# Feed-forward products that read the moving operand in groups of four columns from halves or quarters of the row

## The reference

```python
for layer in range(2):
    h = rmsnorm(x, mix_norm[layer])
    ...                                   # layer 0: gated conv and window attention; layer 1: spatial gating and latent attention
    x = x + y
    h = rmsnorm(x, ffn_norm[layer])
    gate, up = jnp.split(h @ w_ffn_in[layer], 2, axis=-1)      # (512, 1024) @ (1024, 5632)
    x = x + (jax.nn.silu(gate) * up) @ w_ffn_out[layer]        # (512, 2816) @ (2816, 1024)
```

## Time and profile before

| | us |
|---|---|
| median of 2 runs | 1114.61 |
| the runs | 1114.23 and 1114.98 |
| profiled execution: span, first to last instruction | 1112.0 |
| TensorE busy in it | 1102.9 (99%) |
| VectorE, ScalarE, GpSimd busy | 560.2, 420.4, 102.9 |

### The profile page before, as it was taken

How to read it: one execution, slowest core, us unless ns; L and a number is a source line. 1 busy time by engine, 2 the same in 40 slices (tenths; PEclk the granted TensorE clock), 3 DMA queues, 4 the chain that set the end, 5 groups by cost and what they waited for, 6 DMA issues and landing times. The chain is left out here.

```text
span 1112.0 us, 13661 instructions
## 1 busy us (share of the span) xinstructions
PE 1102.9 (99%) x5105; PEld 887.1 (80%) x5105; DVE 560.2 (50%) x784; ACT 420.4 (38%) x662; POOL 102.9 (9%) x126
## 2 busy tenths in 40 slices
PE   8999999999999999999999999999999999999998
PEld 7777788888888888888877766788888888888887
DVE  6678977434433433242466588656433433453321
ACT  5545445333322322231345567544322322332110
POOL 6000000001000100000002023000000100110000
PEclk9999999999999999999999999999999999999999
DMA  7422223333333233322233200223233333327431
GB/s 236 159 57 76 76 75 96 114 95 95 94 94 94 94 102 103 98 95 85 67 103 94 77 35 1 77 96 112 89 101 94 94 97 100 102 78 170 113 123 48
DMA packets 101289, 106.00 MB, mean 95 GB/s; under 512 B 26235, under 2 KB 77888, under 8 KB 101120
## 3 DMA queue, kind: packets, MB, share of 16 engines
q1 hardware_dynamic: 83536, 103.04, 29.8%
q10 hardware_dynamic: 16656, 2.10, 1.1%
q0 software_dynamic: 1056, 0.30, 0.1%
HBM read 101.23 MB, written 2.10 MB: 93 GB/s over the span
## 5 line engine op out<-in xcount | busy, mean ns | idle before, releaser
L1122 DVE TENSOR_TENSOR w_lo<-raw,w_hi 128x1024 fp32r<-128x1024 f32 (+2 forms) x192 | 224.6, 1176 | 419.1 <-ACT w_hi L697 416.3
L697 ACT ACTIVATE w_hi<-raw 128x1024 fp32r<-128x1024 f32 (+2 forms) x192 | 194.2, 1017 | 468.7 <-PE ps L1685 438.4
L1683 PE MATMUL ps<-h_hi,w_hi 128*128 128x512 f32 x912 | 359.7, 394 | 1.0 <-DVE h_lo L1146 1.0
L1685 PE MATMUL ps<-h_hi,w_lo 128*128 128x512 f32 x912 | 355.1, 389 | 0.0
L1684 PE MATMUL ps<-h_lo,w_hi 128*128 128x512 f32 x912 | 355.0, 389 | 0.0
L1683 PEld LDWEIGHTS ps<-h_hi,w_hi 128*128 128x128 f32 x912 | 171.3, 188 | 42.9 <-issue 6.7
L1684 PEld LDWEIGHTS ps<-h_lo,w_hi 128*128 128x128 f32 x912 | 171.2, 188 | 36.7 <-issue 1.7
L1685 PEld LDWEIGHTS ps<-h_hi,w_lo 128*128 128x128 f32 x912 | 171.2, 188 | 35.9
L581 POOL TENSOR_TENSOR ffn_t<-ffn_t,row_scale 128x512 f32<-128x512 f32 x40 | 51.0, 1295 | 614.2 <-ACT ffn_t L883 614.2
L1684 PE MATMUL ps<-w_lo,act_hi 128*128 128x512 f32 (+1 forms) x178 | 68.8, 387 | 0.0
L1685 PE MATMUL ps<-w_hi,act_lo 128*128 128x512 f32 (+1 forms) x178 | 68.8, 387 | 0.0
(11 more groups left out here) (283 smaller groups left out, 1173.4 us busy)
## 6 DMA issues: line engine op xcount, KB each, us to landing
raw<-in_w_ffn_in SPq DMA_DIRECT2D x88, 512.0 KB, 3.5
raw<-in_w_ffn_out SPq DMA_DIRECT2D x44, 512.0 KB, 3.7
raw<-in_e_w_in SPq DMA_DIRECT2D x17, 512.0 KB, 3.7
raw<-in_o_w_in SPq DMA_DIRECT2D x8, 512.0 KB, 3.6
raw<-in_o_w_out SPq DMA_DIRECT2D x8, 512.0 KB, 3.6
raw<-in_e_w_out SPq DMA_DIRECT2D x8, 256.0 KB, 3.9
raw<-in_e_w_out SPq DMA_DIRECT2D x4, 512.0 KB, 4.5
out_tok<-x_blocks ACTq DMA_DIRECT2D x16, 128.0 KB, 2.5
```

What stands on the lines that cost most here:

```text
L697: ins = act.activation(dst, src, ACT.Copy)
L1122: ins = TT(dst, src, high, ALU.subtract)
L1683: MM(dst, st_hi, mv_hi, start=start, stop=False)
L1685: return MM(dst, st_lo, mv_hi, start=False, stop=stop)
```

## The change

The rows of `h_hi` and `h_lo` are stored in another order in rounds 1 and 3, and read back through the same pattern, so that the array gets the columns in the old order. A row of 512 columns is seen as groups of four. In round 1 the groups go in turn to the first and the second half of the row, in round 3 in turn to the four quarters. For feature tiles 0 to 3 the groups run from the end of each half or quarter to its start, for tiles 4 to 7 from its start to its end. `h_order` is the pattern of the stored tile, `x_order` the same columns of `xT` in their own order. The moving operand of a feed-forward input matmul thereby has three levels: 4 columns side by side, a jump of 256 columns (1024 bytes) or 128 columns (512 bytes) to the next half or quarter, and a step of 4 columns up or down. `h_low` is issued once for each half or quarter, with the count of the semaphore on the last.

```diff
--- before.py
+++ after.py
@@ -39,6 +39,7 @@
 RAW_SLOTS = 2
 W_SLOTS = 4
 LEAD = W_SLOTS
+RUNS_BACK = {(1, 0): (2, True), (1, 1): (2, False), (3, 0): (4, True), (3, 1): (4, False)}
 
 
 E_Q, E_KV, E_AIN, E_AC, E_AB, E_OUT = 0, 4, 6, 10, 14, 18
@@ -650,6 +651,21 @@
     def h_gain(rnd, ft):
         return mix0_gain[:, ft:ft + 1] if rnd == 0 else g_col({1: G_FFN0, 2: G_MIX1, 3: G_FFN1}[rnd] + ft)
 
+    def h_order(tile, rnd, ft):
+
+        if rnd not in (1, 3):
+            return tile[:, ft, :]
+        parts, back = RUNS_BACK[rnd, ft // 4]
+        view = tile[:, ft, :].rearrange("p (b a i) -> p a b i", b=parts, i=4)
+        return view[:, ::-1, :, :] if back else view
+
+    def x_order(rnd, ft):
+
+        if rnd not in (1, 3):
+            return xT[:, ft, :]
+        parts, back = RUNS_BACK[rnd, ft // 4]
+        return xT[:, ft, :].rearrange("p (a b i) -> p a b i", b=parts, i=4)
+
     X_BANKS = (4, 5, 6, 7, 4, 5, 6, 7)
     V_BANKS = ((0, 2), (3, 3))
 
@@ -724,7 +740,7 @@
         def h_high(rnd, ft):
 
             act.wait_ge(x_ready, 8 * rnd + ft + 1)
-            act.activation(h_hi[:, ft, :], xT[:, ft, :], ACT.Copy, scale=h_gain(rnd, ft)).then_inc(h_hi_ready, 1)
+            act.activation(h_order(h_hi, rnd, ft), x_order(rnd, ft), ACT.Copy, scale=h_gain(rnd, ft)).then_inc(h_hi_ready, 1)
 
         def h_square(rnd, ft):
             f = 8 * rnd + ft
@@ -1143,8 +1159,15 @@
         def h_low(rnd, ft):
             f = 8 * rnd + ft
             dve.wait_ge(h_hi_ready, f + 1)
-            STT(out=h_lo[:, ft, :], in0=xT[:, ft, :] if rnd else ps[:, X_BANKS[ft], :], scalar=h_gain(rnd, ft), in1=h_hi[:, ft, :].bitcast(F32),
-                op0=ALU.mult, op1=ALU.subtract).then_inc(h_lo_ready, 1)
+            if rnd not in (1, 3):
+                STT(out=h_lo[:, ft, :], in0=xT[:, ft, :] if rnd else ps[:, X_BANKS[ft], :], scalar=h_gain(rnd, ft),
+                    in1=h_hi[:, ft, :].bitcast(F32), op0=ALU.mult, op1=ALU.subtract).then_inc(h_lo_ready, 1)
+                return
+            dst, src, high = h_order(h_lo, rnd, ft), x_order(rnd, ft), h_order(h_hi, rnd, ft).bitcast(F32)
+            for part in range(RUNS_BACK[rnd, ft // 4][0]):
+                ins = STT(out=dst[:, :, part, :], in0=src[:, :, part, :], scalar=h_gain(rnd, ft), in1=high[:, :, part, :],
+                          op0=ALU.mult, op1=ALU.subtract)
+            ins.then_inc(h_lo_ready, 1)
 
         def h_sum(rnd, ft):
             f = 8 * rnd + ft
@@ -1941,7 +1964,8 @@
 
             def half_group(n, j, b0, shift):
 
-                load(n + j, plain(256, 2), range(4 * (j // 2), 4 * (j // 2) + 4), H,
+                load(n + j, plain(256, 2), range(4 * (j // 2), 4 * (j // 2) + 4),
+                     lambda k: (h_order(h_hi, rnd, k), h_order(h_lo, rnd, k)),
                      (b0 + 2 * (j % 2), b0 + 2 * (j % 2) + 1), j < 2, j >= 2, shift)
 
             pe.wait_ge(x_ready, 8 * rnd + 4)
```

## The result

The changed kernel takes 1182.43 us (1182.31 and 1182.55) against 1114.61: ratio 1.0608, 95% interval 1.0577 to 1.0639, slower by 67.8 us. The span of its profiled execution is 1180.5 us, 68.5 over the one before.

What follows compares the result with a forecast made beforehand. TensorE, busy 99% of the 1112.0 us span, was taken as the bound. Zero for reads, `h_high` and clock plus 1.2 us for the `h_low` split, on the 1114.6 us median, gave 1115.8 us, own range 1113.8 to 1119.

Steps and rivals of the forecast that it cites:

- The read in groups of four: Main term, TensorE's 2112 feed-forward input matmuls: jumps in the moving read cost zero, bounded between a 28 us gain and +427 us.
- The signs of being wrong: Spacings differing between layers or tile directions, longer `h_high`, VectorE fixed part far from 0.13 us, or idle time inside groups.
- The argument from the spacing: TensorE matmul starts: 0.417 ns a column, one cycle at 2.4 GHz, plus fixed 0.0133 us; no delay inside a contiguous row.
- rival C: TensorE's moving reads: alternating halves hide some of the fixed 13.3 ns, all of it 28 us, giving 1088 us; chance 0.03.
- rival A: All 2112 matmuls: read port bubbles at jumps; one cycle each +113 us, 1229 us, or 1172 if half pay; chance 0.15.
- The split of `h_low`: VectorE: each extra piece pays 0.13 us (to 0.21) fixed; the sum is +1.2 us, ends 0 and +3.8.
- the hole at the mean of layer 1: TensorE waits 1.1 us before `mean` in layer 1's second half, as `h_low` pieces delay VectorE's last sum; high price 2.9.
- a semaphore's passage: 0.1 us added to the 1.1 us hole in the `h_low` split's sum of +1.2 us.
- `h_high`: ScalarE's 16 writes at permuted places: same count and elements, 0.72 us each, cost zero; even +0.3 us each is hidden.
- The clock: Granted clock 1.00 in both feed-forward stretches; values unchanged, only storage moves: zero.
- Rival B: Start of each matmul costs a few ns more, not growing with columns; 1119 to 1130 us; chance 0.05.

Runs made afterwards that it cites:

- e_turn1: Changed kernel with all h_hi and h_lo rows of layers 0 and 1 read as single columns in turn from two halves, forward: 1093.9 us, ratio 0.982 to kernel before.
- e_n256: Changed kernel with feed-forward input matmuls on the first 256 columns only; halves by four, plain, single columns from halves, quarters by four: 983.86 us.
- e_sweep: Changed kernel with groups of four, forward, from 8 and 16 parts (layer 0), 32 and 64 parts (layer 1): 1156.05 us.
- e_width: Changed kernel with forward groups of 8 and 16 columns, from halves in layer 0 and quarters in layer 1: 1135.77 us.
- e_split: Kernel before with only h_low cut into two (layer 0) or four (layer 1) instructions, rows in old order: 1115.53 us against 1114.39, ratio 1.001.
- e_best: Changed kernel with single columns from halves for h_hi and h_lo, plus act_hi and act_lo rows of layer 0's output products: 1088.35 us, ratio 0.9769 to kernel before.
- e_near: Changed kernel with single columns in turn from two neighbouring runs of 4 and 2 columns (layer 0), 8 and 64 (layer 1): 1098.73 us.
- e_swap: Changed kernel with directions exchanged: tiles 0 to 3 forward, 4 to 7 backward: 1181.32 us.
- e_ldw64: Changed kernel with 64 stationary columns instead of 128; layer 0 quarters and halves by four forward, layer 1 plain: 1149.18 us.
- e_wstep: Changed kernel with weights read every second column of 256; halves by four, plain, single columns from halves, quarters by four: 1151.33 us.
- e_step2: Changed kernel with every second column and backward singles from halves (layer 0), backward pairs from halves and backward groups of four from 32 parts (layer 1): 1282.45 us.
- e_back1: Changed kernel without halves or quarters: tiles 0 to 3 read backward in groups of four, tiles 4 to 7 plain: 1121.55 us.

## Why the prediction was wrong

**The step that failed is the main term**, "The read in groups of four": I took zero for 2112 matmuls, and it measured +21.7 ns (halves) and +42.0 ns (quarters) each, 67.3 us. The reason given, that all words of a group lie side by side and each is read once, is true and not what counts. The nearest rows were of other engines, at 64 columns a run, as the text said; the error was to let them and that reason set the value where the trace had nothing of its own. The signs of being wrong that the prediction named came true: the spacings differ between halves and quarters, and between backward and forward.

**The argument from the spacing was too strong.** The earlier trace rows do show 0.417 ns for each further column of a plain row, and 13.3 ns that don't grow with the columns. I took 0.417 ns for the length of one cycle (2.4 GHz is its inverse) and concluded that nothing is lost inside a row; that was an estimate from this one difference. From it I concluded that nothing in the fixed 13.3 ns depends on addresses (rival C) and that moving on to the next four columns is free wherever they lie (against rival A). Both fell: single columns from two streams take 10.8 of the 13.3 ns away (e_turn1), and e_n256 shows the groups' price growing with the columns, from 6.7 to 23.5 ns for halves.

**Rival A is the nearest to the case**, with 0.15. Its place holds: all 2112 matmuls pay, in the read of the moving operand. Its mechanism, one lost step at every jump, does not: groups of four 64 bytes apart jump as often and pay nothing (223.4 ns, e_sweep), and halving the jumps of quarters takes nine tenths of their price away (from 41.2 to 4.4 ns, e_width). Its price was mis-sized too, since I let it begin at a column's whole 0.417 ns for every jump (1229 us, or 1172 for half the forms). Spread over the 128 jumps, the price is 0.17 ns a jump for halves (21.7 by 128) and 0.33 for quarters (42.0 by 128). That the measured 1182 lies near the 1172 is chance: all forms pay, each less than 0.417 ns a jump.

**The split of `h_low`** was right in its working: 0.13 us a piece forecast, 0.13 measured (0.39 for three more pieces); +1.2 us forecast, +1.1 alone; the hole at the mean of layer 1 forecast at 1.1 us, 0.99 found. The 0.1 us that the sum adds for a semaphore's passage came from no row; in e_split the last sum of squares ends at 760.67 us and the mean starts at 760.82, 0.15 us later. In the full change that hole is covered, and no cost of the split is seen on TensorE. **`h_high`** at zero was right (722 ns, 719 before). **The clock** at 1.00 was right.

**Rival B**, a fixed start price of the three-level pattern, is not the case: the pattern costs nothing at 64 bytes (223.4 ns), and the price grows with the columns (halves 6.7 ns with 256, 23.5 with 512).

**Rival C**, the alternating reads that hide the fixed part, was dismissed at 0.03 for this change, rightly, since groups of four from halves and quarters don't bring it (246.5 to 269.4 ns); but a gain out of the fixed part exists: e_turn1 and e_best measure 10.8 ns of the 13.3. That two parts of the memory answering in turn make it is not shown; 16 bytes between the streams are enough (215.8 ns, e_near).

What is shown: the price is that of TensorE's moving read (21.7 and 42.0 ns a matmul, 67.3 of 67.8 us), it goes with the form of the pattern, rises with the columns (e_n256), and isn't the split (1.1 us, e_split), the tile (e_swap) or the weight load alone (e_ldw64, e_wstep). What stays open: why groups of four range from 223.4 (64 bytes apart) over 226.7 (plain) and 250 (1024) to 276 ns (256), why quarters are worse than halves with groups of four and better with 8, why single columns take 216.0 ns from halves, 283.6 from quarters and 486.7 from 8 parts, and how the weight load comes in. So the cause inside the read stays open.

## What to carry to other kernels

In a stream of matmuls that keeps TensorE busy, the address pattern of the moving operand has a price of its own: here the same 512 columns took from 215.8 to 486.7 ns a matmul. It is not seen by counting elements or bytes: measure the form, with distances between starts, before building on it. For float32 rows at full clock, storing them so that single columns come in turn from two places (even 16 bytes apart, a permutation within eight columns) was 5% faster than the plain row (215.8 against 226.7 ns). Of the other ways of jumping that were measured, groups of four 64 bytes apart were 1.5% faster forward (223.4) and level backward (227.0), single columns inside one 16-byte group were level (227.5), and all the rest were slower (231.1 ns and up). Where a profile has no row for an access, its price is unknown, and 0.15 for the case that it costs was too little.

## What was not expected of the hardware

- A row of 512 float columns read plainly isn't the fastest form measured here: 226.7 ns against 215.8 for single columns from two streams, both with 128 weight columns loaded each time.
- Every second column, two uses for each 16 bytes, takes 450.8 ns a matmul, twice a plain row (e_step2).
- A weight load of 64 columns in place of 128 makes plain rows slower, 230.0 against 226.7 ns; weights read with a step of two columns, 233.2 (e_ldw64, e_wstep).
- Reading downwards in groups of four costs 6.7 ns a matmul (e_back1), but from halves it is 3.6 ns cheaper than upwards (246.6 against 250.2, e_swap).
- ScalarE and VectorE wrote and read the groups of four at their usual durations, within 1%: `h_high` 722 ns on the mean (719 before), VectorE's pieces of 128 and 256 columns 343 and 479 ns, 345 and 479 when contiguous (e_split).
